# Dense matmuls that read and write their columns from the last to the first

## The reference

```python
h = rms_norm(x);  u = h @ w_in                  # first block: sparse attention and an RWKV recurrence
y = gate0 * (o_nsa @ proj_nsa) + gate1 * (o_rwkv @ proj_rwkv)
x = x + y @ w_out
x = x + conv_ffn(rms_norm(x), ffn_up, ffn_conv, ffn_down)
x = x + 0.5 * rms_norm(swiglu(rms_norm(x), w_gate, w_up, w_down))        # second block
x = x + rms_norm(hybrid_mixer(...))             # dilated attention and an mLSTM, w_in_2, two branches, w_out_2
x = x + 0.5 * rms_norm(swiglu(rms_norm(x), ...))
```

## Time and profile before

| what | value |
|---|---|
| median of 3 runs | 2433.51 us (2431.32 to 2433.78) |
| profiled execution | 2431.45 us |
| its span, first to last instruction | 2429.6 us |
| PE busy | 2378.4 us, 98% of the span |
| DVE, ACT, POOL busy | 1065.1, 935.4, 1034.3 us |
| mean granted TensorE clock | 0.992 of 2.4 GHz |
| HBM read | 200.76 MB, 83 GB/s with what is written |

### The profile page before, as it was taken

How to read it: one execution, slowest core, us unless ns; L and a number is a source line. 1 busy time by engine, 2 the same in 40 slices (tenths; PEclk the granted TensorE clock), 3 DMA queues, 4 the chain that set the end, 5 groups by cost and what they waited for, 6 DMA issues and landing times.

```text
span 2429.6 us, 38821 instructions
## 1 busy us (share of the span) xinstructions
PE 2378.4 (98%) x13906; PEld 1953.2 (80%) x13906; DVE 1065.1 (44%) x1843; ACT 935.4 (38%) x1278; POOL 1034.3 (43%) x754
## 2 busy tenths in 40 slices
PE   8999998899999999999999999999999999999999
PEld 6878777778888888888888877888888888888887
DVE  4456475455555522222222855763333448222212
ACT  3345432243555533444423322224444624444322
POOL 3322230035454555455555633443333355555554
PEclk9999999999999999999999999999999999999999
DMA  5211110023232233222233322221222232222332
GB/s 159 70 44 44 61 62 3 3 92 98 87 96 99 99 104 104 95 95 95 95 106 109 101 70 70 86 80 62 87 78 78 70 104 69 95 95 97 102 104 95
DMA packets 60732, 204.21 MB, mean 84 GB/s; under 512 B 10940, under 2 KB 11708, under 8 KB 60380
## 3 DMA queue, kind: packets, MB, share of 16 engines
q1 hardware_dynamic: 55152, 196.45, 24.7%
q10 hardware_dynamic: 5488, 6.44, 0.9%
HBM read 200.76 MB, written 2.10 MB: 83 GB/s over the span
## 4 chain that ended last, share of the span: by engine, by line
PE 87%; DVE 9%; issue 2%; ACT 1%; POOL 1%; DMA 0%; SPq 0%; DVEq 0%; ACTq 0%
PE psum L403 85%; DVE rope_t L2540 2%; DVE qk_st L2539 2%; POOL x L388 1%; PE psum L650 1%; DVE rope_t L2532 1%; DVE qk_st L2542 1%; PE psum L1090 0%; DVE inv L2157 0%; DVE tmp L2458 0%; ACT dd L1437 0%; DVE a_t L2098 0%; PE psum L772 0%; DVE zm L1799 0%; DVE h_lo L1833 0%
## 5 line engine op out<-in xcount | busy, mean ns | idle before, releaser
L376 POOL TENSOR_TENSOR w_lo<-raw,w_hi 128x512 fp32r<-128x512 f32 x732 | 1006.3, 1396 | 1377.3 <-ACT w_hi L1243 1377.3
L403 PE MATMUL psum<-h_hi,w_hi 128*128 128x512 f32 x2128 | 852.8, 401 | 13.7 <-DVE h_lo L1833 10.6
L403 PE MATMUL psum<-h_lo,w_hi 128*128 128x512 f32 x2128 | 835.4, 393 | 0.0
L1243 ACT ACTIVATE w_hi<-raw 128x1024 fp32r<-128x1024 f32 x366 | 386.1, 1055 | 684.7 <-PE psum L403 669.0
L403 PE MATMUL psum<-h_hi,w_lo 128*128 128x512 f32 x2128 | 535.4, 390 | 0.0
L403 PEld LDWEIGHTS psum<-h_hi,w_hi 128*128 128x128 f32 x2128 | 403.5, 190 | 112.4 <-issue 26.6
L403 PEld LDWEIGHTS psum<-h_lo,w_hi 128*128 128x128 f32 x2128 | 403.5, 190 | 83.6 <-issue 3.2
L403 PEld LDWEIGHTS psum<-h_hi,w_lo 128*128 128x128 f32 x2128 | 399.0, 188 | 83.9 <-issue 0.5
L1799 DVE TENSOR_TENSOR tmp<-psum,rst 128x512 f32<-128x512 f32 x100 | 69.1, 691 | 322.5 <-PE psum L403 322.2
L403 PE MATMUL psum<-hid_hi,w_hi 128*128 128x512 f32 x528 | 205.4, 389 | 0.0
L403 PE MATMUL psum<-hid_lo,w_hi 128*128 128x512 f32 x528 | 205.4, 389 | 0.0
(11 more groups left out here) (427 smaller groups left out, 2605.1 us busy)
## 6 DMA issues: line engine op xcount, KB each, us to landing
raw<-in_w SPq DMA_DIRECT2D x366, 512.0 KB, 3.3
x<-in_x SPq DMA_DIRECT2D x4, 512.0 KB, 6.3
x<-in_x ACTq DMA_DIRECT2D x1, 2048.0 KB, 7.9
out_y<-x SPq DMA_DIRECT2D x8, 256.0 KB, 2.3
mask<-in_mask ACTq DMA_DIRECT2D x1, 1536.0 KB
tmp<-in_cmp_w ACTq DMA_DIRECT2D x2, 512.0 KB, 5.7
masks<-in_masks ACTq DMA_DIRECT2D x1, 768.0 KB, 4.3
lora<-in_lora ACTq DMA_DIRECT2D x1, 512.0 KB, 3.2
```

The lines of the kernel that those rows point to most:

```text
L376: pool.tensor_tensor(w_lo[:, g.slot, part], raw[:, g.slot, part], w_hi[:, g.slot, part].bitcast(F32), ALU.subtract).then_inc(sem("lo_ready ...
L403: return pe.matmul(out, lhsT, rhs, start=start, stop=stop)
L1243: act.activation(w_hi[:, g.slot], raw[:, g.slot], ACT.Copy).then_inc(sem("hi_ready"), 1)
```

## The change

The two helpers of the dense matmuls pass the moving operand (hi, lo) and the output with their columns reversed, `[:, ::-1]`. Column j of the product still lies in word j of the bank. The stationary operand (w_hi, w_lo) is passed as before, and so are all other matmuls. The instructions of every engine, their order and their waits are the same as before, PE's 3568 rows of the program among them (loops counted once); in the program as built the two patterns of a dense matmul start at column 511 with a step of -1 where they started at 0 with a step of 1.

```diff
             def mm_hi(out, slot, k, hi, lo, start):
                 a = w_hi[:, slot, tok(k)]
-                mm(out, a, hi, start, False)
-                mm(out, a, lo, False, False)
+                mm(out[:, ::-1], a, hi[:, ::-1], start, False)
+                mm(out[:, ::-1], a, lo[:, ::-1], False, False)

             def mm_lo(out, slot, k, hi, stop):
-                return mm(out, w_lo[:, slot, tok(k)], hi, False, stop)
+                return mm(out[:, ::-1], w_lo[:, slot, tok(k)], hi[:, ::-1], False, stop)
```

## The result

The changed kernel takes 2481.82 us (median of 4 runs, 2480.87 to 2482.28), the kernel before 2433.65 us beside it. The ratio is 1.0197, with a 95% interval from 1.018 to 1.0215: 2% slower, 48.2 us. The forecast was no change, 2433.5; the time lies in the stated range, between its two likely cases, and nearest to the rival called a small toll (2494), which had a chance of 0.06.

A forecast was written before the change was run, and what follows sets the result against it. PE's 8640 dense matmuls at about 226.7 ns were taken to bound the kernel. The profiled 2431.45 us plus 8550 x 0 gave 2431.45, as a median 2433.5 us; range 2425 to 4190.

The forecast's parts named there:

- the stated range: Whole kernel: 2425 to 4190 us, meant to hold 8 in 10, from no change to a little above half speed.
- its two likely cases: Whole kernel: no change, 2433.5 us, chance 0.56; or one word per two cycles, about 4160 us, chance 0.30.
- small toll: Dense matmuls: each stream charged some nanoseconds at its ends, 7.3 ns x 8550 = 62 us, 2494 us; chance 0.06.
- What bounds the kernel, and by how much: PE's 8640 dense matmuls, 1959 of 2429.6 us; one nanosecond on each adds 8.6 us, almost undiminished.
- I take p = 0: Dense matmuls: p, the extra price of a descending 512-column stream at full clock, taken as zero over 8550 matmuls.
- the row of the tiles 513 words apart: Projection (pj_in): eight matmuls at 234 ns each, 7 more than elsewhere; taken as showing odd-word starts read at full rate.
- Uses the same two-word and four-word groups: Moving read: descending from word 511 uses each group completely before the next, so it should cost nothing extra.
- Rigid, which reads like a fixed count of cycles rather than a race with memory: Feed-forward matmuls (hid_hi): all 389 ns over 528, taken as support for no extra price.
- untouched: Dense matmuls' weight loads: same patterns and same count as before, so no change in cost expected from them.
- Half rate: Dense matmuls: descending stream passes one word per two cycles, 203 ns more each, 1736 us, about 4160 us; chance 0.30.

## Why the prediction was wrong

The second point below rests on two rows of the kernel before, from its output projection (PE in order of time, as the earlier trace rows):

```profile
579.24 0.39 PE L403 MATMUL psum<-y_hi,w_hi 128*128 128x512 f32 x1
...
580.83 0.39 PE L403 MATMUL psum<-y_lo,w_hi 128*128 128x512 f32 x1
```

- What bounds the kernel, and by how much: right. A nanosecond per dense matmul is 8.6 us; 48.2 us is 5.6 ns on the mean over 8640, 6.6 where they stand alone. No other engine changed its work, and nearly the whole loss fell on the path.
- The step that failed is "I take p = 0", by the row of the tiles 513 words apart. The row was the right one and the reading of it wrong. It showed 234 ns where 227 is usual for columns that differ in nothing but their place, and I took from it that the columns are read at the full rate and set the 7 ns aside as stray values of straight code. But the projection stands in a loop in the program (of two units, run four times). All its dense matmuls stand so (median 233 ns), while the output projection right behind it, a loop of the same kind with its tiles at multiples of 64 words, runs at 227 (the rows above: seven distances in 1.59 us). In loops with no other engine at work the same ascending read costs 235.3 at word 1 and 233.2 at word 2. So the place of the read has a price, and p was not 0 but 6.6 ns. That the row's 7.3 comes so near is partly luck: in the loops a start off the multiple of 64 costs from 2.4 (word 16) to 8.6 ns (word 1).
- The small toll, the rival nearest in time, had the wrong mechanism: nanoseconds charged to each stream at its ends would be the same at every length, and a descent costs 4 ns at 384 columns, nothing at 448 and 320, and less than nothing at 256.
- "Uses the same two-word and four-word groups": true, and not the scale that counts. Swapped pairs are free, blocks of 4 and 16 words in descending order cost as much as a whole descent, blocks of 64 nothing.
- "Rigid, which reads like a fixed count of cycles rather than a race with memory": a false alternative. The recorded length is as rigid after, at 397 ns, and in the loops 226.7 and 233.3 ns are each held for a whole loop, so an even pace says nothing about whether a read costs more.
- The weight loads "untouched": true of their instructions (188 ns each, before and after), but their place is part of the arrangement. In before's program each weight block, and each moving tile but those of the projection, stands at a multiple of 64 words; moving the weights alone costs 1.8%.
- The small toll was priced at 62 us, 7.3 ns for 8550 matmuls at before's best pace. It is 48: at 6.6 ns the same sum gives 56, and in the mixed stages before was already above its best pace.
- Half rate: refuted for the descent, with the write free and the read at 233 ns. It is near what a step of two words costs (453 ns). So a step of +1 is not needed to stay off the half rate: swapped pairs are free, words two apart are not.
- The write into the bank costs nothing, descending (ratio 1.0004) or with swapped pairs (226.7 ns). The Trainium skill, "PSUM — Partial Sum Buffer", Specifications, would have non-contiguous patterns slow a matmul; taken as a step of +1 the runs speak against it, taken as two words sharing a line they agree. The read of every second fp32 word costs 453 ns, and a descending read 6.6 ns more than an ascending one. For the read the Trainium skill, "SBUF — State Buffer" (the note on SBUF cachelines), makes two hits on a 16-byte line enough; every second word gives two, and a descent gives four. The measurements decide against both readings, that such a step is free and that a descent is.

What stays open is why a descent did not settle at 226.7 ns in any of the places tried. That the descending read is what costs, and that the place of either read matters on a scale of 64 words, is shown. That the two reads get in each other's way is argued from this and not shown: the toll stays when the weight load shrinks to two columns, and no run moves both reads together.

## What to carry to other kernels

When one row of a trace differs from the rest in just the respect that a change is about, its difference is the first estimate, even where it is small and looks like noise: multiply it by the count, and see whether the row's whole stage shows it, before setting it aside. For dense streams of F32R matmuls, keep moving tiles and weight blocks at multiples of 64 words and read the moving tiles upwards, at least in whole blocks of 64; the output may be written from its last word to its first. Before a loss is put down to a direction, move the addresses without it and see whether the loss comes too.

## What the runs showed of the hardware that was not expected

- Distances between F32R matmuls of 512 columns at the full clock come to 226.7 or 233.3 ns in most loops, and to 240.0 in some; these are 8.5, 8.75 and 9 times the 26.7 ns of 64 columns at 2.4 GHz. Other places gave means in between (229.1 with the read from word 16, 232.5 with the weights from word 32), as several distances take turns.
- Which value holds can depend on what ran just before: 233.3 or 236.7 ns for one and the same loop.
- bf16 operands show no toll of direction: 216 ns either way; other places were not tried with them.
- A step of two fp32 words on the moving read doubles the cost (453 ns); with bf16 operands a step of two elements costs 226 in place of 216 ns.
